# The three feed-forward ends of a two-block layer: order of the residual, the root chain, the column sums, and where the attention bias is laid out

## The reference

```python
def first_block(x, c, ctx, c_ctx, ...):      # gated linear attention and convolution, then a feed-forward
    sh1, sc1, gt1, sh2, sc2, gt2 = split(silu(c) @ w_ada + b_ada, 6)
    ...
    x = x + gt1 * mix_l
    x = x + gt2 * swiglu(modulate(rmsnorm(x, g_ffn), sh2, sc2), w_ffn_in, w_ffn_out)
    return rmsnorm(x, g_final)

def second_block(x, c, positions, ...):      # feed-forward, attention mixer, feed-forward
    sh1, sc1, g1, sh2, sc2, g2, sh3, sc3, g3 = split(silu(c) @ w_ada + b_ada, 9)
    x = x + 0.5 * g1 * swiglu(modulate(rmsnorm(x, ffn1_norm), sh1, sc1), ffn1_w_in, ffn1_w_out)
    ...                                      # chunk attention adds rel_bias[rel] to its scores
    x = x + g2 * (merged @ w_out)
    x = x + 0.5 * g3 * swiglu(modulate(rmsnorm(x, ffn2_norm), sh3, sc3), ffn2_w_in, ffn2_w_out)
    return rmsnorm(x, final_norm)
```

## Time and profile before

| | us |
|---|---|
| median of three runs (lowest, highest) | 1171.85 (1169.42, 1174.54) |
| profiled execution, its own time | 1168.47 |
| its span | 1166.5 |
| TensorE busy in the span | 1124.3 (96%) |
| VectorE busy | 857.7 (74%) |
| ScalarE busy | 569.5 (49%) |
| GpSimd busy | 68.9 (6%) |
| mean granted clock of TensorE | 0.985 of full |

### The profile page before, as it was taken

One profiled execution on the slowest core, in us unless ns is written; L12 is line 12 of the kernel. 1 busy time (PEld: TensorE's weight loads), 2 busy tenths in 40 slices (PEclk: granted clock), 3 DMA queues, 4 the chain that ended last, 5 costly groups with the idle time before them and its releaser, 6 DMA issues.

```text
span 1166.5 us, 19146 instructions
## 1 busy us (share of the span) xinstructions
PE 1124.3 (96%) x7764; PEld 1019.4 (87%) x7764; DVE 857.7 (74%) x1082; ACT 569.5 (49%) x729; POOL 68.9 (6%) x132
## 2 busy tenths in 40 slices
PE   3999999999999999999899999999999999999996
PEld 2899988999999888888688888889999999888885
DVE  1578776897877787877778777878777776755676
ACT  3495433544434544444445454446655545444442
POOL 4000000100000000000300000011000001000000
PEclk8899999999999999999899999999999999999999
DMA  9934554698965587778538777747865654655770
GB/s 284 302 101 144 186 177 145 181 289 274 299 204 184 192 270 261 263 237 297 186 119 279 253 253 262 240 153 234 280 191 182 220 176 151 226 183 188 236 242 37
DMA packets 192548, 250.28 MB, mean 215 GB/s; under 512 B 4860, under 2 KB 171967, under 8 KB 192351
## 3 DMA queue, kind: packets, MB, share of 16 engines
q1 hardware_dynamic: 183838, 216.92, 57.1%
q0 software_dynamic: 8640, 32.38, 8.4%
HBM read 248.23 MB, written 1.05 MB: 214 GB/s over the span
## 4 chain that ended last, share of the span: by engine, by line
PE 88%; DVE 7%; SPq 2%; ACT 1%; issue 1%; DMA 1%; POOL 0%; POOLq 0%; DVEq 0%; ACTq 0%
PE twin L1278 86%; DVE wlo L1888 2%; DVE arena L1896 2%; DVE arena L1888 1%; DMA arena<-in_w_ada 1%; PE twin L1339 1%; DVE X L1888 1%; SPq L517 1%; PE twin L1604 1%; ACT arena L853 1%; ACT whi L853 0%; SPq L567 0%; DVE A_both L1888 0%; PE twin L1725 0%; PE twin L1392 0%
## 5 line engine op out<-in xcount | busy, mean ns | idle before, releaser
L1278 PE MATMUL twin<-A_both,whi 128*128 128x256 f32 (+1 forms) x2208 | 579.8, 340 | 4.4 <-DVE A_both L1888 3.3
L1888 DVE TENSOR_TENSOR wlo<-raw,whi 128x2048 fp32r<-128x2048 f32 x169 | 386.7, 2289 | 116.9 <-ACT whi L853 116.6
L1278 PE MATMUL twin<-A_both,wlo 128*128 128x256 f32 x1632 | 437.5, 281 | 0.0
L853 ACT ACTIVATE whi<-raw 128x2048 fp32r<-128x2048 f32 x169 | 323.2, 1912 | 205.8 <-PE twin L1278 204.4
L1278 PEld LDWEIGHTS twin<-A_both,whi 128*128 128x128 f32 x2208 | 371.2, 190 | 46.9 <-issue 9.5
L1278 PEld LDWEIGHTS twin<-A_both,wlo 128*128 128x128 f32 x1632 | 310.2, 190 | 11.3 <-DVE A_both L1888 0.4
L1896 DVE SCALAR_TENSOR_TENSOR arena<-ada_raw,arena 128x256 f32<-128x256 f32 (+2 forms) x322 | 167.3, 520 | 15.5 <-issue 1.7
L853 ACT ACTIVATE arena<-twin 128x512 f32<-128x512 f32 (+5 forms) x167 | 88.4, 555 | 115.6 <-PE twin L1278 85.5
L853 ACT ACTIVATE arena<-arena 128x512 f32<-128x512 f32 (+7 forms) x132 | 69.8, 558 | 145.4 <-DVE arena L1888 114.3
L1278 PE MATMUL twin<-whi,B_hi 128*128 128x512 f32 (+2 forms) x340 | 126.8, 373 | 0.2 <-DVE B_lo L1888 0.2
L1278 PE MATMUL twin<-wlo,B_hi 128*128 128x512 f32 (+2 forms) x340 | 125.3, 368 | 0.0
(11 more groups left out here) (132 smaller groups left out, 898.0 us busy)
## 6 DMA issues: line engine op xcount, KB each, us to landing
raw<-in_w_in SPq DMA_DIRECT2D x48, 1024.0 KB, 5.7
raw<-in_ffn_w_in SPq DMA_DIRECT2D x44, 1024.0 KB, 5.1
ada_raw<-in_w_ada POOLq DMA_DIRECT2D x28, 1024.0 KB, 6.4
ada_raw<-in_w_ada SPq DMA_DIRECT2D x24, 1024.0 KB, 5.4
raw<-in_w_ffn_in SPq DMA_DIRECT2D x22, 1024.0 KB, 5.1
raw<-in_ffn_w_out SPq DMA_DIRECT2D x22, 1024.0 KB, 4.9
raw<-in_w_ffn_out SPq DMA_DIRECT2D x11, 1024.0 KB, 4.9
arena<-in_w_ada SPq DMA_DIRECT2D x8, 1024.0 KB, 11.6
```

The lines of the kernel that those rows point to most:

```text
L853: return nc.scalar.activation(o, i, f, **kw)
L1278: return nc.tensor.matmul(o, l, r, start=start, stop=stop, **kw)
L1888: return nc.vector.tensor_tensor(o, x, y, op)
```

## The change

The residual stands directly behind the gate row. The split that stood between them is cut in two parts, of 768 and 1280 columns, that stand before and behind the norm's low parts. This holds for the first two ends; at the last end there was no unit left to split. `twice_norm` is rewritten, so that behind the last square one addition and the power remain. At the last end the multiplication by the gains leaves the residual: the upper half of the columns is multiplied after it, and the lower half within the output's own scaling. The column sums use 32 columns of ones, and their readers take every 32nd column of the bank. The bias copy becomes eight copies of 128 x 256, each of which waits for a step of block two's first feed-forward.

```diff
@@ GpSimd, twice_norm
                 for t in range(TT):
                     p = [part8[:, 2 * t + x:2 * t + x + 1] for x in range(2)]
                     g = [part8[:, 4 + 2 * t + x:4 + 2 * t + x + 1] for x in range(2)]
+                    q = rstd[:, 12 + t:13 + t]
                     pool.wait_ge(sq_piece, 2 * t + 1)
                     link(nc.gpsimd.tensor_scalar(p[0], p[0], EPS, None, ALU.add))
+                    link(nc.gpsimd.tensor_scalar(q, p[0], EPS, None, ALU.mult))
                     pool.wait_ge(sqg_piece, 2 * t + 1)
+                    link(nc.gpsimd.tensor_tensor(g[0], g[0], q, ALU.add))
                     pool.wait_ge(sq_piece, 2 * t + 2)
+                    link(nc.gpsimd.tensor_scalar(q, p[1], EPS, None, ALU.mult))
+                    link(nc.gpsimd.tensor_tensor(g[0], g[0], q, ALU.add))
+                    pool.wait_ge(sqg_piece, 2 * t + 2)
+                    link(nc.gpsimd.tensor_tensor(g[1], g[1], g[0], ALU.add))
+                    negative_root(rstd[:, 6 + t:7 + t], g[1]).then_inc(rstd_done, 1)
+                for t in range(TT):
+                    p = [part8[:, 2 * t + x:2 * t + x + 1] for x in range(2)]
                     link(nc.gpsimd.tensor_tensor(p[0], p[0], p[1], ALU.add))
-                    link(nc.gpsimd.tensor_scalar(p[1], p[0], EPS, None, ALU.mult))
-                    link(nc.gpsimd.tensor_tensor(p[1], p[1], g[0], ALU.add))
-                    pool.wait_ge(sqg_piece, 2 * t + 2)
-                    link(nc.gpsimd.tensor_tensor(p[1], p[1], g[1], ALU.add))
-                    negative_root(rstd[:, 6 + t:7 + t], p[1]).then_inc(rstd_done, 1)
-                for t in range(TT):
                     negative_root(rstd[:, 12 + t:13 + t], part8[:, 2 * t:2 * t + 1]).then_inc(frs_done, 1)
@@ GpSimd, bias copy
             pool.wait_ge(u_in, 16)
-            link(nc.gpsimd.tensor_copy(U, Ur.rearrange("p (k h) -> p h k", h=H2)[:, :, ::-1]))
+            for h in range(H2):
+                pool.wait_ge(lo_ready, BASE_FFN[1] + 6 + 3 * h)
+                link(nc.gpsimd.tensor_copy(U[:, h, :], Ur.rearrange("p (k h) -> p h k", h=H2)[:, h, ::-1]))
@@ ScalarE, output
-                act.wait_ge(xg_piece, 4 + 2 * t + 2)
+                act.wait_ge(xg_piece, 4 + t + 1)
@@ TensorE, shift_and_scale (KW = 32)
-                        ins = mm(bank[b][:, KD * x + k:KD * x + k + 1], acc[:, c:c + P], one, True, True)
+                        o = KW * (KD * x + k)
+                        ins = mm(bank[b][:, o:o + KW], acc[:, c:c + P], ones[:, 0:KW], True, True)
@@ VectorE, new
+            def split_part(u, part):
+                dve.wait_ge(hi_ready, u + 1)
+                cs = slice(0, 3 * UC) if part == 0 else slice(3 * UC, KD * UC)
+                ins = rest(wlo[ring(u)][:, cs], raw[ring(u)][:, cs], whi[ring(u)][:, cs])
+                if part:
+                    ins.then_inc(lo_ready, 1)
@@ VectorE, columns
-                    sh, sc = bank[b][:, 0:KD], bank[b][:, KD:2 * KD]
+                    sums = bank[b][:].rearrange("p (k w) -> p k w", w=KW)[:, :, 0]
+                    sh, sc = sums[:, 0:KD], sums[:, KD:2 * KD]
@@ VectorE, end of ffn
                 gate_row(r)
                 dve.wait_ge(gr_done, r + 1)
-                split(u0 + 3 * NF + 1)
...
-                        if f != 1:
+                        if f == 0:
                             dve.wait_ge(x_piece, 4 * f + j + 1)
-                            tt(yF[j], X[:, t, cs], finrow[f // 2][:, cs], ALU.mult).then_inc(xg_piece, 1)
+                            tt(yF[j], X[:, t, cs], finrow[0][:, cs], ALU.mult).then_inc(xg_piece, 1)
@@ VectorE, output_rows
+                dve.wait_ge(x_piece, 12)
+                for t in range(TT):
+                    tt(xg[:, t, 512:D], X[:, t, 512:D], finrow[1][:, 512:D], ALU.mult).then_inc(xg_piece, 1)
                 for t in range(TT):
                     dve.wait_ge(frs_done, 2 + t + 1)
-                    dve.wait_ge(xg_piece, 4 + 2 * t + 1)
-                    ts(XN[:, t, 0:512], xg[:, t, 0:512], rstd[:, 14 + t:15 + t], None, ALU.mult).then_inc(out_done, 1)
+                    dve.wait_ge(sq_piece, 8 + 2 * t + 1)
+                    stt(XN[:, t, 0:512], X[:, t, 0:512], rstd[:, 14 + t:15 + t], finrow[1][:, 0:512], ALU.mult,
+                        ALU.mult).then_inc(out_done, 1)
@@ VectorE, main program
             columns(3, column_bank(3), VEC["ffn1_norm_2"], bias_col(3), (0,))
+            split_part(BASE_FFN[1] + 1, 0)
             norm_low(3)
+            split_part(BASE_FFN[1] + 1, 1)
             scaled_rows()
...
             columns(4, column_bank(4), VEC["mix_norm_2"], bias_col(4), (0,))
+            split_part(BASE_P2 + 1, 0)
             norm_low(4)
+            split_part(BASE_P2 + 1, 1)
             second()
```

More of the change, by code:

```diff
@@ L35 @@
 RING = 3
+KW = 32
 Q0, K0, V0, G0, DD0 = 0, 512, 1024, 2048, 3072
```

## The result

The changed kernel took 1158.86 us in median (1158.70 to 1159.01) against 1171.8 for the kernel before beside it; the ratio is 0.9895, with a 95% interval from 0.9875 to 0.9915. By the ratio that is 12.3 us or 1.05% faster; the two medians lie 12.9 apart. (A fourth execution of the changed kernel took 1590.11 us at a mean granted clock of 0.653; it was in a slow state and is left out.)

A forecast was written before the change was run, and what follows sets the result against it. TensorE was taken as the bound, nearly nine tenths of the last chain. Terms 5.03 + 1.4 + 0 + 0 + 1.4 = 7.8 us took the profiled 1168.47 to 1160.6, carried to a median of 1164.0; range 1159.5 to 1168.0.

The forecast's parts named there:

- Bias copy, 3.00: Block one's feed-forward end: with GpSimd's attention bias copy moved away, VectorE's held subtraction shortens and the first product comes 3.00 us earlier.
- the clock behind it, 1.4: First products after block one's feed-forward: TensorE's clock at full instead of half once the 2.87 us idle goes, gaining 1.4 us.
- Residual first, 2.03: End of block one's feed-forward: without the 2.29 us weight split ahead of it, the residual starts and ends 2.03 us earlier.
- Root chain, 0.1: GpSimd's root work in the norm after block one's feed-forward: fewer operations behind the last square save 0.1 us, within 0 to 0.5.
- First end as a whole, 5.03: End of block one's feed-forward: the next feed-forward's first product at 580.35 instead of 585.38, 5.03 us gained, including the copy's 3.00.
- 32-column sums, 0: Column sums in the norms: wider passes cost nothing, at most 0.3 us a norm; a kept clock was possible but counted as 0.
- Second end, net 0: End of block two's first feed-forward: at most 0.72 us gained, taken back by a later stall; 1.0 net if the clock kept.
- The stall: Third unit of block two's second mixer: its split ends at 792.4 against a demand at 791.8, stated as 0.7 us lost.
- Last end, 1.4: End of block two's second feed-forward, which ends the program: last store issued 1.4 us earlier, within 1.0 to 2.0.
- The first, that the sums hold the clock: Rival: 32-column sums keep TensorE's clock at two later norms, adding 1.0 and 1.1; gain 9.9, time 1161.9 us, chance 0.33.
- The idle that only moves: Rival: roots stay held, the third unit stalls longer, first products' clock stays down; gain 5.0, time 1166.9 us, chance 0.19.
- No piece of the copy held anything: Judges the slower rival: bias copy pieces in block two's first feed-forward delay VectorE's multiplication; time 1178.4 us, chance 0.04.

## Why the prediction was wrong in size

**The step that failed** is the last one of the sum: "It is 3.4 below the median of the three runs, 1171.85, to which I carry the difference: 1164.0". It took the distance between a profiled execution and the median of three for a property of the program that the changed one would share. The changed kernel's profiled execution stands 0.15 above its median. Of the 5.1 us between forecast and result this is 3.5 (3.4 and the 0.15). The other 1.6 is the difference between 1160.6, forecast for the profiled execution, and its 1159.01; it comes from a second step, the clock at the second end, which was put at nothing.

The runs show what the 3.4 was, and it is two things. The larger part, 2.1, is the draw: the median of 83 executions of the kernel before is 1169.7, and the three happened to give 1171.85. Against 1169.7 the profiled 1168.47 is only 1.25 low. That rest is a property of the kernel before, which takes anything from 1167.6 to 1175.1 by the norms at which the clock falls; its profile was one of the short executions. The nine executions of the changed kernel take 1158.7 to 1160.7. With the 32-column sums alone the spread falls from 7.5 to 3.7, with the copy in pieces alone to 3.6 (1.3 but for one execution). With one column again the changed kernel spreads over 3.3, with the copy whole again over 3.2, with the first split put back over 3.2. So no single edit has that steadiness: the sums and the shorter idles share it. The steadier clock is worth 0.8 us by the medians (1169.7 less 1159.4, against the pair's 9.46) and 1.9 by the means. I had in hand three times from 1169.42 to 1174.54 and did not read their spread of 5.1 us as a warning, either that their median was a loose one or that the change could take some of it away.

**The terms, one by one.**

- *Bias copy, 3.00, and the clock behind it, 1.4:* right. The place shows 4.29 when the edit stands alone; the timings say 5.2 alone (3.4 to 7.0 by the interval) and 4.9 undone. That the excess is the steadier clock fits the closer executions but isn't shown. The clock's 1.4 is not there in every execution: in the changed kernel's second profile it stood at 0.53 at 580 to 582, where the first products run, and of the 1.38 only 0.77 is left (186.01 us from first product to next sums, 185.40 in the first profile and 186.78 before). A piece was taken for 0.50 and takes 0.68, inside its bound and without effect.
- *Residual first, 2.03:* right at its place (2.03 on TensorE, 2.02 on VectorE). The medians show 1.1 and don't settle it.
- *Root chain, 0.1:* it is 0.30 at VectorE, inside the bounds.
- *First end as a whole, 5.03:* 4.83.
- *32-column sums, 0:* the cost was right (3.65 against 3.62 us a norm), the worth was not. "Whether the wider sums keep it, no row shows", and I took the end of the bound that the full passes before the 2.87 us idle suggested. Those passes say only that a following idle of 2.87 us loses the clock; the norms in question have an idle of 0.72 or none. Over the executions it is worth 2.4 to 3.1. One of its places the prediction did not price: the norm behind mixer one, where one column lost the clock in three of five profiles, at up to 2.65 us, and wider sums in none of eleven.
- *Second end, net 0:* gained 2.13 (0.86 ahead of the turns and 1.27 behind their start, at the kept clock), given back 0.59 at the third unit and 0.72 up to the next sums. So the net was 1.4 to 1.5, which is most of the 1.6 above. The stall was foreseen with its cause, that everything up to ScalarE's split behind the sines comes later; its own terms give 0.6 (792.4 against 791.8), not the 0.7 that it states. What failed was that only the sums were thought of as a means to keep the clock here. The early residual does most of it, by closing the idle: lost in six of six profiles with the late residual, kept in eight of ten with the early one, once even with one column. In the changed kernel's second profile, where the clock fell, the stretch gains 0.55 and the net is the forecast's nothing.
- *Last end, 1.4:* 1.30.

**The rivals.** The first, that the sums hold the clock, is right in part. They do at the norm behind mixer one, and at times behind block two's mixer. At the second end, where the rival puts 1.0 of its 2.1, the early residual has the larger share. In each of the changed kernel's two profiles one of these two later norms kept the clock and the other lost it. That its gain of 9.9 lies near the pair's 9.46 is therefore partly luck, and its time of 1161.9 is 3.0 too long for the same carrying to the median. The idle that only moves was wrong but for the third unit: the roots' wait did not grow, and in the first profile the clock was at 0.94 and above from the first products on (in the second they began at half clock and lost about half of the 1.4). No piece of the copy held anything.

**Do the terms add up?** Against 1159.59, the undone edits cost 4.9 (copy), 2.4 (sums), 1.1 and 0.85 (splits) and 0.5 (roots); with 1.30 for the last end this makes 11.0. The two timings of the whole give 12.3 and 10.5 (0.991 of about 1169). The terms thus account for the whole within what was measured. Against the median of all 83 executions of the kernel before the whole is 10.3. How much of the sums' and the copy's parts is the same steadiness, counted in whichever is undone, stays open: alone the sums are worth about 2 us (0.2 to 3.6 by the interval), undone 2.4 to 3.1.

## What to carry to other kernels

Forecast a change in the execution that you can see, and look at how the times scatter before carrying it to the median: a scatter of half a per cent in a kernel bound by TensorE was the clock falling at different places. Three timings of such a kernel put its median 2.1 us too high here, a fifth of the gain. Look for a lone VectorE instruction that takes eight times its usual time (3.43 us for 0.43) beside a copy on GpSimd; here it was the largest single term, and moving the copy cost nothing. Passes that cost the same but carry more columns are free to try (3.62 to 3.66 us from 1 to 128 columns). An idle of TensorE's, even one of 0.7 us, is worth closing for the clock behind it as well as for itself. One that can't be closed can be filled; but fill it with TensorE's own work, not by moving VectorE's work into a step that has no slack.

## What was not expected of the hardware

- Float32 sums with 1, 32 and 128 columns took 3.62, 3.65 and 3.66 us for 16 products. Yet the wider sums kept the clock more often: at the norm behind mixer one in eleven of eleven profiles against two of five, and behind block two's mixer in none of five with one column, three of seven with 32 and four of four with 128.
- One program differed by up to 7.5 us between executions while TensorE's work was the same. The page TensorE: Matmul & The Clock Gate of the Trainium skill, Part 1, says that the chip's watch on TensorE runs freely and isn't restarted by a kernel, so that the point of a change varies; the pair of profiles with 1.95 and 3.65 us for the same turns agrees with it.
- At the first end the clock of the changed kernel fell about where the 32-column sums end: in one profile in the window of their last products (0.85 at 572 to 574, the sums end at 573.6), in the other in the idle behind them (1.00 at 572 to 574, 0.77 at 574 to 576). Behind the 128-column sums it stood at 1.00 through the idle of 1.58 us that follows, and fell in the second one (0.57 at 576 to 578). With seven warm products in the first idle it stayed at 1.00 through the second, of 0.96 us, in all three profiles that have them.
